# Attention bias added on VectorE to negated scores, in place of an identity product on TensorE

## The reference, cut to what matters

```
qg = (q * (dh ** -0.5)).reshape(bsz, heads, rows, GRID_W, dh)
s_win = jnp.einsum('bhrqd,bhrkwd->bhrqkw', qg, kg) + bias
s_win = jnp.where(col_mask[:, None, :], s_win, NEG_INF)
s_ctx = jnp.einsum('bhrqd,bhld->bhrql', qg, k_ctx)
pr = jax.nn.softmax(jnp.concatenate([s_win, s_ctx], axis=-1), axis=-1)
o = p_win @ v_win + p_ctx @ v_ctx
```

## Time and profile before

| what | value |
|---|---|
| median of the runs (lowest, highest) | 1883.53 us (1882.77, 1887.25) |
| the profiled execution, its own time | 1887.33 us |
| its span, from the first to the last instruction | 1885.6 us |
| mean granted TensorE clock over the span | 0.936 |
| TensorE busy | 1694.1 us, 90% |
| VectorE busy | 1122.5 us, 60% |
| ScalarE busy | 923.1 us, 49% |
| latent units of the attention | 774.3 to about 850.9 us |
| context units of the attention | 850.9 to about 873 us |

### The profile page before, as it was taken

How to read it: one execution, slowest core, us unless ns; L and a number is a source line. 1 busy time by engine, 2 the same in 40 slices (tenths; PEclk the granted TensorE clock), 3 DMA queues, 4 the chain that set the end, 5 groups by cost and what they waited for, 6 DMA issues and landing times.

```text
span 1885.6 us, 21382 instructions
## 1 busy us (share of the span) xinstructions
PE 1694.1 (90%) x7965; PEld 1314.2 (70%) x7965; DVE 1122.5 (60%) x1030; ACT 923.1 (49%) x962; POOL 75.6 (4%) x62
## 2 busy tenths in 40 slices
PE   4897888699999699999859999999999999999991
PEld 2343443588888599875458888888888888878781
DVE  1207401433333562343368898979797979797976
ACT  3033110433322422221227686868686868686864
POOL 1000000000000020000000000000000000000001
PEclk9888889799999899997859999999999999999996
DMA  9665469343323451500429899999999999999994
GB/s 329 246 240 195 180 243 385 103 134 127 102 85 134 98 148 56 206 7 1 151 94 354 304 396 349 396 348 396 347 396 350 396 349 396 349 396 349 396 349 147
DMA packets 253307, 472.76 MB, mean 251 GB/s; under 512 B 32349, under 2 KB 84281, under 8 KB 253257
## 3 DMA queue, kind: packets, MB, share of 16 engines
q1 hardware_dynamic: 230128, 438.33, 64.4%
q10 hardware_dynamic: 19272, 20.56, 3.2%
q0 software_dynamic: 3856, 13.18, 1.9%
HBM read 454.17 MB, written 17.86 MB: 250 GB/s over the span
## 4 chain that ended last, share of the span: by engine, by line
PE 75%; DVE 9%; DMA 5%; ACT 4%; issue 3%; ACTq 2%; POOL 0%; DVEq 0%; SPq 0%; POOLq 0%
PE ps L1872 26%; PE ps L1885 11%; PE ps L1671 10%; PE ps L1635 5%; PE ps L1688 5%; PE ps L1535 4%; PE ps L1727 3%; DMA ring<-in_w_in_dram 3%; DVE e_lo L1397 2%; PE ps L1650 2%; ACT e_hi L1025 2%; PE ps L1742 2%; ACTq L899 2%; PE ps L1794 1%; PE ps L1560 1%
## 5 line engine op out<-in xcount | busy, mean ns | idle before, releaser
L1397 DVE TENSOR_TENSOR e_lo<-e_raw,e_hi 128x2048 fp32r<-128x2048 f32 (+1 forms) x330 | 690.7, 2116 | 117.6 <-ACT e_hi L1025 114.3
L1025 ACT ACTIVATE e_hi<-e_raw 128x2048 fp32r<-128x2048 f32 (+1 forms) x330 | 580.6, 1774 | 127.4 <-PE ps L1872 90.5
L1872 PE MATMUL ps<-e_hi,e_x 128*128 128x512 f32 (+1 forms) x1728 | 511.4, 376 | 7.2 <-DVE e_x L1492 7.2
L1872 PEld LDWEIGHTS ps<-e_hi,e_x 128*128 128x128 f32 x1728 | 316.6, 189 | 66.9 <-issue 10.9
L1872 PE MATMUL ps<-e_lo,e_x 128*128 128x512 f32 (+1 forms) x864 | 321.9, 373 | 0.0
L1885 PE MATMUL ps<-e_hi,e_h 128*128 128x512 f32 x792 | 221.7, 391 | 0.0
L1872 PEld LDWEIGHTS ps<-e_lo,e_x 128*128 128x128 f32 x864 | 163.4, 189 | 27.1
L1671 PE MATMUL ps<-split,hi_x 128*128 128x512 f32 (+1 forms) x576 | 172.3, 384 | 4.8 <-DVE lo_x L1284 4.8
L1885 PEld LDWEIGHTS ps<-e_hi,e_h 128*128 128x128 f32 x792 | 147.5, 188 | 29.6
L1885 PE MATMUL ps<-e_lo,e_h 128*128 128x512 f32 x396 | 122.1, 390 | 0.0
L1635 PE MATMUL ps<-hn_t,ring 128*128 128x386 f32 x320 | 113.9, 518 | 8.8 <-DMA ring<-in_w_in_dram 8.8
(11 more groups left out here) (248 smaller groups left out, 1857.2 us busy)
## 6 DMA issues: line engine op xcount, KB each, us to landing
e_raw<-in_moe_w_gate_dram SPq DMA_DIRECT2D x94, 1024.0 KB, 10.6
e_raw<-in_moe_w_up_dram SPq DMA_DIRECT2D x92, 1024.0 KB, 11.1
e_raw<-in_moe_w_down_dram SPq DMA_DIRECT2D x90, 1024.0 KB, 11.0
ring<-in_w_mod_dram SPq DMA_DIRECT2D x36, 1024.0 KB, 9.9
mod_extra<-in_w_mod_dram SPq DMA_DIRECT2D x12, 1024.0 KB, 13.1
ring<-in_w_qkv_dram SPq DMA_DIRECT2D x6, 2048.0 KB, 8.8
ring<-in_w_in_dram SPq DMA_DIRECT2D x5, 2048.0 KB, 16.7
ring<-in_ffn_w_gate_dram SPq DMA_DIRECT2D x10, 1024.0 KB, 8.0
```

The costliest lines, as they stand in the source:

```text
L1025: act.activation(high_part(c), raw(c), ACT.Copy).then_inc(hi_ok, 1)
L1397: dve.tensor_tensor(low_part(c), raw(c), high_part(c).bitcast(F32), ALU.subtract).then_inc(lo_ok, 1)
L1872: ins = pe.matmul(out, e_x[:, xt, ci, :], wt[:, kk, :], start=(ci == 0 and m == 0), stop=(ci == KC - 1 and m == 2))
```

## The change

The scores are computed negated: the queries are scaled by -1/8 rather than 1/8. The table `outside` gets the sign turned (+1e30 outside the window), and GpSimd computes outside - bias, so that the tile `bias` holds the negated bias with the mask. The identity product is left out. On VectorE a latent unit now takes first the minimum of the 128 context scores into `ctx_min`; then one combined instruction adds the bias tile to the 256 latent scores in PSUM, in place, and takes the minimum over them, starting from `ctx_min`, into `nmx`. The exponential gets scale -1. The wait for `bias_ok` moves from TensorE to VectorE. Context units take a minimum in place of a negated maximum.

```diff
-    k[:, C_NEG:C_NEG + GRID_W] = np.where(inside, 0.0, NEG)
+    k[:, C_NEG:C_NEG + GRID_W] = np.where(inside, 0.0, -NEG)
...
+        ctx_min = at(o + 3 * D + 48, 2, 1)
...
-            pool.tensor_tensor(bias, bias, outside, ALU.add).then_inc(bias_ok, 1)
+            pool.tensor_tensor(bias, outside, bias, ALU.subtract).then_inc(bias_ok, 1)
...
-                        act.activation(q_t[:, m, 0:P], ps[:, n % 6, 0:P], ACT.Copy, scale=HD ** -0.5)
+                        act.activation(q_t[:, m, 0:P], ps[:, n % 6, 0:P], ACT.Copy, scale=-HD ** -0.5)
...
-                act.activation(p_buf[:, u % 3, 0:n], ps[:, u % 2, 0:n], ACT.Exp, bias=nmx[:, u % 2, :],
+                act.activation(p_buf[:, u % 3, 0:n], ps[:, u % 2, 0:n], ACT.Exp, bias=nmx[:, u % 2, :], scale=-1.0,
                                accum_out=sums[:, t, h:h + 1]).then_inc(p_ok, 1)
...
+            dve.wait_ge(bias_ok, 1)
             for u, (t, h) in enumerate(units):
                 n = 384 if t else P
                 dve.wait_ge(sc_ps, u + 1)
-                dve.tensor_reduce(nmx[:, u % 2, :], ps[:, u % 2, 0:n], AX_X, ALU.max, negate=True).then_inc(max_ok, 1)
+                if t:
+                    j0 = 6 * h + 2 - 2 * (t - 1)
+                    ordered(dve.tensor_reduce(ctx_min[:, u % 2, :], ps[:, u % 2, 256:384], AX_X, ALU.min))
+                    near = ps[:, u % 2, 0:256]
+                    dve.tensor_tensor_reduce(near, near, bias[:, j0:j0 + 4, :].rearrange("p a b -> p (a b)"), 1.0,
+                                             ctx_min[:, u % 2, :], ALU.add, ALU.min, nmx[:, u % 2, :]).then_inc(max_ok, 1)
+                else:
+                    dve.tensor_reduce(nmx[:, u % 2, :], ps[:, u % 2, 0:n], AX_X, ALU.min).then_inc(max_ok, 1)
                 if u >= 2:
                     prob_turned(u - 2)
...
             pe.wait_ge(ctx_ok, 1)
-            pe.wait_ge(bias_ok, 1)
...
                 if t:
-                    j0 = 6 * h + 2 - 2 * (t - 1)
-                    pe.matmul(ps[:, u % 2, 0:256], ident, bias[:, j0:j0 + 4, :].rearrange("p a b -> p (a b)"),
-                              start=True, stop=False)
-                    pe.matmul(ps[:, u % 2, 0:256], q, kk_t[r:r + 64, ci, S0:W], start=False, stop=True)
+                    pe.matmul(ps[:, u % 2, 0:256], q, kk_t[r:r + 64, ci, S0:W], start=True, stop=True)
                     ins = pe.matmul(ps[:, u % 2, 256:384], q, kc_t[r:r + 64, ci, :], start=True, stop=True)
```

More of the change, by code:

```diff
@@ L970, in _ @@
                     else:
-                        act.activation(q_t[:, m, 0:P], ps[:, n % 6, 0:P], ACT.Copy, scale=HD ** -0.5)
+                        act.activation(q_t[:, m, 0:P], ps[:, n % 6, 0:P], ACT.Copy, scale=-HD ** -0.5)
                         act.activation(by_tile(q_t[:, m, S0:W]), reverse(ps[:, n % 6, S0:W]), ACT.Copy,
-                                       scale=HD ** -0.5).then_inc(qk_ok, 1)
+                                       scale=-HD ** -0.5).then_inc(qk_ok, 1)
                 if n + 4 < 16:
@@ L1337, in _ @@
                     else:
-                        dve.tensor_scalar(q_t[:, m, 0:P], ps[:, n % 6, 0:P], HD ** -0.5, None, ALU.mult)
-                        dve.tensor_scalar(by_tile(q_t[:, m, S0:W]), reverse(ps[:, n % 6, S0:W]), HD ** -0.5, None,
+                        dve.tensor_scalar(q_t[:, m, 0:P], ps[:, n % 6, 0:P], -HD ** -0.5, None, ALU.mult)
+                        dve.tensor_scalar(by_tile(q_t[:, m, S0:W]), reverse(ps[:, n % 6, S0:W]), -HD ** -0.5, None,
                                           ALU.mult).then_inc(qk_dve, 1)
```

## The result

The changed kernel takes **1925.5 us**, the median of four executions (1907.3 to 1927.3). The kernel before, run beside it, takes 1883.2 us (1881.6 to 1887.3). The ratio is 1.020, with a 95% interval of 1.014 to 1.026. The forecast was 1869 us: the change loses 42 us where 14 were to be gained. The profiled execution of the changed kernel took 1927.3 us, with a span of 1925.7 and a mean granted clock of 0.907.

What follows compares the result with a forecast made beforehand. TensorE's own sequence was taken to set the latent units' pace. Removing the identity product saves 14.8 us, less 0.5 for stalls, 14.3; from the median of 1883.5 that gives 1869 us, range 1862 to 1877.

Steps and rivals of the forecast that it cites:

- What the removed product is worth: Latent units on TensorE: first two gain nothing, unit 2 gains 0.63 us, the other 29 gain 0.49 each; together 14.8.
- Rival C: Latent units: TensorE's clock falls because it does less in every round; slower, 1890 us; chance 0.06.
- 0.49 us saved a unit: Latent units: values to scores takes 0.81 us against 1.30, so the round becomes 1.94 us.
- the 0.5 us subtracted for stalls at u = 20 and 23: Dividing a tile keeps VectorE busy beyond its slack: 0.4 us of stall at u = 20, 0.1 at u = 23.
- The 0.33 us of "issue": TensorE's idle pause before the latent keys' 64-row weight loads, forecast to stand behind the values' 128-row loads afterwards.
- VectorE at 0.93 us: Latent units: minimum 0.29, wait 0.03, combined instruction 0.42, write-out 0.19; fits beside TensorE's work.
- B: VectorE becomes the bound: combined instruction at the scan's rate, 0.96 us, round 2.11 us, 1876.6 us; chance 0.12.
- The gain goes through to the end: Projection and experts hang on the attention's last copy, so the saving is carried to the end.
- E: Context units and start of projection: the clock's fall doesn't come, some 7 us more, 1862 us; chance 0.07.

Runs made afterwards that it cites:

- the first fill: The changed kernel with four useless identity products (256 columns) in TensorE's wait in front of unit 2: 1870.4 us, ratio 0.9926.
- the burst: The changed kernel with twelve useless products in a row in front of the transposes of unit 6, the wait at unit 2 left: 1888.9 us.
- the run with the wait in the middle: The kernel with four useless products before unit 2, plus seven ordered ScalarE copies before unit 14's exponential, so TensorE waits at unit 16: 1885.2 us.
- the early table load: The changed kernel with the exponential's table load taken early and one output transfer's issue moved behind the fourth exponential: 1913.3 us.

## Why the prediction was wrong

**The step that failed** is in "What the removed product is worth": the table load ends when it ends, so the first two units "gain nothing", and TensorE starts unit 2 at the same point "in either kernel". The restart was right to the hundredth, 0.74 us behind the load. What the step didn't ask is what TensorE does in the meantime. The removed products were a large part of what it did, and they kept the scores of units 0 and 1 apart; without them the wait grew from 0.35 to 2.25 us. I priced that idle time at nothing, and even counted a gain of 0.63 us on its account. With it the clock fell, and 42 us went.

**Rival C** named the right mechanism, with the wrong cause and place. It asked whether a thinner round holds the clock, and answered that "TensorE stays without gaps". The thin rounds do hold it (the first fill, the burst), and most of the gap to come could have been worked out from the start: weight loads idle for 0.54 us, and two products of 0.63 less in front of them. Its size was also too small: a unit at 0.50 takes 3.57 us, not 3.3, and nearly all 30 ran so, not half. As for its sentence on the Trainium skill (TensorE: Matmul & The Clock Gate, "Part 4: PE-mode transpose"), that transposes don't count for the clock: the fill's latent units, with three transposes in every round, run at 1.00, which doesn't settle it, since they have products too.

**What was right**, by the kernels in which the wait is covered:
- 0.49 us saved a unit and a round of 1.94: measured 1.94. These weight loads and matmuls of the fill stand where its first context unit and its output projection start:

```profile
831.12 0.29 PEld L1774 LDWEIGHTS ps<-work 64*128 64x128 f32 x2
...
861.70 43.71 PE L1659 MATMUL ps<-ring,hn_t 128*128 128x512 f32 x96 [1.32 <-DVE hn_t L1374]
```

  From the restart to the first context unit the fill takes 58.5 us (831.12 - 772.59) where the kernel before took 73.2. That is 14.7 us saved, of 14.8 forecast; the 0.5 us subtracted for stalls at u = 20 and 23 don't show, since TensorE's matmuls wait for no other engine behind the restart. From there to the projection it takes 30.6 us (861.70 - 831.12) where the kernel before took 27.8, so 2.7 are lost again: the clock falls sooner in the context units, to 0.50 in the window from 839 to 850 us, 8 us behind the first of them, where in the kernel before it was still at 1.00 from 858 to 863.8, up to 13 us behind. The range had 2 us for this.
- The reason given for the 0.49 us was wrong, though the number was right. The 0.33 us of "issue" does not move behind the values: their last load ends at 801.04 (800.29 + 0.75), and the next starts at 801.10. The number held because the 0.81 us were read whole, at a junction of the same kind.
- VectorE at 0.93 us, in time for everything: measured 0.87, and 0.66 us idle before each minimum where 0.45 was forecast. The combined instruction is 0.49 against the 0.42 taken, the write-out 0.14 against 0.19. B's 0.96 is excluded.
- The gain goes through to the end: 1870.4 and 1870.9 us were measured where 1869 was forecast.
- E, the context units at the full clock, was right as a mechanism and nearly in its size (some 7 us forecast, 5.9 measured, from 1870.4 to 1864.5), but in no run did it come by itself; it took thirteen products.

**What the runs leave open.** Why the clock came back after some 27 us behind the wait at unit 16, and not within 120 us behind the wait at unit 2, was not found. Eight transposes in a row, those of a finished tile, stand just ahead of the return in the run with the wait in the middle (first row), and also just ahead of the short return of the changed kernel at 900.2 us (second row):

```profile
828.62 1.91 PE L1547 MATMUL ps<-k_sb,xn 128*128 128x128 f32 x8
```

```profile
897.12 1.91 PE L1544 MATMUL ps<-k_sb,xn 128*128 128x128 f32 x8
```

In the changed kernel eight such transposes at 849.62 us raised nothing, so they are not enough by themselves. Nor does any run show why equal programs went two ways at 1.19 us. A kernel with a short wait and no added work on TensorE wasn't tried: the early table load got down to 1.73 us.

## What to carry to other kernels

Before work is taken from TensorE, look for each wait for which that work was the cover, the first and last rounds of a loop above all, and ask what the work kept apart: the pause can grow by more than the work removed (1.90 us for 1.26 here). A pause of some 2 us there can cost far more than itself, since it can lower the clock for much of what follows (a wait of 2.35 us cost 72 us in the kernel before). Read the granted clock beside the busy share; a TensorE that is busy in 102 of 102 us may be at half speed. Where such a pause can't be removed, a few useless products in it are cheap: four of them were worth 55 us here.

## What the runs showed of the hardware

- With a wait of 2.25 us on TensorE in dense work the clock went from 1.00 to 0.50, as it did with 1.62, 1.73, 2.35 and 2.52 us in the executions profiled. With 0.32 and 0.35 us it didn't. The kernel whose profiled execution waited 1.19 us kept its time in two executions of four. These are readings of these places, not a limit of the chip.
- The score products of units 0 and 1, each on 64 rows, ran at the same time once nothing stood between them: 0.93 us for both.
- At 0.50 the clock stayed for over 100 us of work without a gap, with the identity product in the units as well as without it. The Trainium skill (TensorE: Matmul & The Clock Gate, "Part 1: The HAM clock gate (the "warmup" mystery)") says that activity releases the throttle; by the busy column the trace disagrees, 102.00 of 102.00 us at 0.50. In the burst kernel the clock rose within twelve 128x256 products in a row.
- At the lower clock a whole unit takes nearly twice as long, though VectorE and ScalarE keep their pace: it went from 1.94 to 3.57 us, 1.84 times, and in the kernel before from 2.43 to 4.54, 1.87 times.
- The combined add and minimum over 128x256, in place in PSUM, takes 0.49 us, and 0.14 us for writing the minima out.
